# First modulation and input projection cut into quarters of the features, with idle products around them, and a new order of the early weight loads

## The reference, cut to what matters

```python
cond = jax.nn.silu(c)
mod = (cond @ ada_w + ada_b)[:, None, :]                  # ada_w is 1024 x 6144
sh1, sc1, g1, sh2, sc2, g2 = jnp.split(mod, 6, axis=-1)
h = rms_norm(x, ln1_g) * (1.0 + sc1) + sh1                # 256 x 1024
z = h @ w_in                                              # w_in is 1024 x 2840
...                                                       # attention on heads of z, then @ w_out
x = x + g1 * hybrid_mixer(...)
h = rms_norm(x, ln2_g) * (1.0 + sc2) + sh2
x = x + g2 * sparse_moe(h, ...)                           # 32 experts, top 4
```

## Time and profile before

| | |
|---|---|
| median of 3 runs | 1793.73 us (1792.29 to 1797.49) |
| the profiled execution, own time | 1794.16 us |
| its span | 1792.1 us |
| TensorE (PE) busy | 1720.9 us, 96% |
| DVE, ACT, POOL busy | 701.0, 264.4, 132.2 us |
| mean granted TensorE clock | 0.998 |
| DMA | 548.11 MB, mean 306 GB/s |

### The profile page before, as it was taken

How to read it: one execution, slowest core, us unless ns; L and a number is a source line. 1 busy time by engine, 2 the same in 40 slices (tenths; PEclk the granted TensorE clock), 3 DMA queues, 4 the chain that set the end, 5 groups by cost and what they waited for, 6 DMA issues and landing times.

```text
span 1792.1 us, 25082 instructions
## 1 busy us (share of the span) xinstructions
PE 1720.9 (96%) x10167; PEld 1057.6 (59%) x10168; DVE 701.0 (39%) x1280; ACT 264.4 (15%) x534; POOL 132.2 (7%) x188
## 2 busy tenths in 40 slices
PE   7999999999999999999999999999999999999998
PEld 4456543333333333333333333797899998899987
DVE  2655422122122121212212122664578545768743
ACT  1135211011010010101101010214111001511100
POOL 4006400000000001001010010200100000010000
PEclk9999999999999999999999999999999999999999
DMA  9988999969999999999999999741254443535440
GB/s 318 358 277 264 388 415 428 428 283 428 429 428 429 427 428 428 429 429 427 428 429 429 429 427 426 262 160 48 95 184 146 171 159 118 200 142 188 159 171 24
DMA packets 95507, 548.11 MB, mean 306 GB/s; under 512 B 6002, under 2 KB 9282, under 8 KB 68722
## 3 DMA queue, kind: packets, MB, share of 16 engines
q1 hardware_dynamic: 95298, 546.93, 76.0%
q10 hardware_dynamic: 144, 0.26, 0.0%
HBM read 546.12 MB, written 1.05 MB: 305 GB/s over the span
## 4 chain that ended last, share of the span: by engine, by line
PE 76%; DMA 19%; SPq 1%; ACT 1%; issue 1%; DVE 1%; POOL 0%; DVEq 0%; POOLq 0%; ACTq 0%
DMA ring<-in_exp_w 18%; PE ps L1312 18%; PE ps L1556 11%; PE ps L1343 8%; PE ps L1585 6%; PE ps L1626 5%; PE ps L1370 4%; PE ps L1444 4%; PE ps L971 2%; PE ps L1277 2%; PE ps L1264 2%; PE ps L1185 2%; PE ps L1655 2%; PE ps L944 1%; PE ps L1680 1%; ACT sq L1700 1%
## 5 line engine op out<-in xcount | busy, mean ns | idle before, releaser
L1312 PE MATMUL ps<-ring,sq 128*64 128x512 f32 x2112 | 464.4, 593 | 24.0 <-DMA ring<-in_exp_w 24.0
L1312 PEld LDWEIGHTS ps<-ring,sq 128*64 128x64 f32 x2112 | 146.9, 137 | 316.9 <-issue 264.0
L1343 PE MATMUL ps<-arena,sq 128*64 128x512 f32 x1056 | 233.9, 595 | 3.5
L2301 DVE TENSOR_SCALAR sq<-arena,rstd 128x64 f32<-128x64 f32 x68 | 19.5, 330 | 365.2 <-PE ps L1312 364.5
L1343 PEld LDWEIGHTS ps<-arena,sq 128*64 128x64 f32 x1056 | 75.3, 137 | 140.8 <-issue 140.5
L2374 DVE TENSOR_SCALAR hn<-ps 128x512 f32<-128x512 f32 x33 | 22.8, 692 | 318.6 <-PE ps L1312 318.6
L1807 ACT ACTIVATE sq<-hn 128x512 f32<-128x512 f32 x33 | 20.8, 629 | 528.0 <-DVE hn L2374 528.0
L1700 ACT ACTIVATE sq<-ps 128x512 f32<-128x512 f32 (+1 forms) x99 | 51.9, 524 | 308.7 <-PE ps L1343 212.2
L1556 PE MATMUL ps<-arena 128*128 128x136 f32 (+1 forms) x768 | 90.0, 277 | 0.0
L1556 PEld LDWEIGHTS ps<-arena 128*128 128x128 f32 x768 | 88.6, 191 | 0.0
L1700 ACT ACTIVATE arena<-ps 128x512 f32<-128x512 f32 (+4 forms) x68 | 33.4, 501 | 275.9 <-PE ps L1585 78.4
(11 more groups left out here) (418 smaller groups left out, 2240.1 us busy)
## 6 DMA issues: line engine op xcount, KB each, us to landing
ring<-in_exp_w SPq DMA_DIRECT2D x123, 2048.0 KB, 21.2
arena<-in_exp_w SPq DMA_DIRECT2D x68, 2048.0 KB, 19.4
ring<-in_mlp_w_up SPq DMA_DIRECT2D x16, 2048.0 KB, 7.5
ring<-in_mlp_w_down SPq DMA_DIRECT2D x16, 2048.0 KB, 7.8
ring<-in_ada_w SPq DMA_DIRECT2D x8, 2048.0 KB, 12.2
ring<-in_sb_w_qkv SPq DMA_DIRECT2D x6, 2048.0 KB, 14.5
ring<-in_w_in SPq DMA_DIRECT2D x5, 2048.0 KB, 12.2
ring<-in_ada_w SPq DMA_DIRECT2D x8, 1024.0 KB, 9.7
```

The costliest lines, as they stand in the source:

```text
L1312: last = mm(bank(2 + part)[64 * h:64 * h + 64, :], lhs, w[:, k % 2, at:at + 512], start=False, stop=(k == C - 1))
L1343: last = mm(bank(3)[64 * h:64 * h + 64, :], m.aT[:, q, 64 * half:64 * half + 64], w[:, q, 512 * h:512 * h + 512], start=(half == 0 and q = ...
```

## The change

The first modulation is computed by quarters of its columns (q = 0 to 3), each over all 1024 rows: a quarter gives scale and shift of 256 features, two chunks. Its products move 128 columns, where they moved 256. The load `mod q` brings two times 1024 rows of 256 columns. The projection's first 1304 columns (v = 0 to 5) are made by the same quarters of the features: load `inq q` holds 256 rows of `w_in` with 1304 columns, and the six banks stay open over the four quarters. Around this stand 19 idle products of the identity with itself (two before c, eight before x, four before the first modulation, two and three around its turn). VectorE instead of ACT copies the turned x out of PSUM, and ACT loads its table for the square root ahead of the squares.

The loads behind are reordered. Of group 1, parts 0 to 2 are still added up on VectorE, one after each of the third, fourth and fifth chunk of heads; part 3 goes to TensorE in `modulation_sum(1)`, in bank 1, and that sum with its turn (bank 2) moves behind `cw2`. `score(0)` now waits for the result of group 1.

```diff
-A_LOADS = ([("mod", 0, 0), ("mod", 0, 1), ("in", 0, 0), ("mod", 0, 2), ("mod", 0, 3)]
-           + [("in", 0, 1), ("in", 0, 2), ("ada", 1, 0), ("ada", 1, 1), ("in", 0, 3), ("ada", 1, 2), ("in", 0, 4),
-              ("ada", 1, 3), ("in", 0, 5), ("cmp", 0, 0)] + [("ada", 2, k) for k in range(4)] + [("wout", 0, h) for h in range(2)])
+QUARTERS = 4
+IN_FIRST = 1304
+A_LOADS = ([(kind, 0, q) for q in range(QUARTERS) for kind in ("mod", "inq")]
+           + [("in", 0, 3), ("ada", 1, 0), ("in", 0, 4), ("ada", 1, 1), ("in", 0, 5), ("cmp", 0, 0), ("ada", 1, 2),
+              ("ada", 1, 3)] + [("ada", 2, k) for k in range(4)] + [("wout", 0, h) for h in range(2)])
-MOD_BANK, MOD_TURN_BANK = (6, 7, 7), (5, 7, 7)
+MOD_BANK, MOD_TURN_BANK = (6, 1, 7), (5, 2, 7)
...
+    if kind == "inq":
+        return ("in_first", c + 1) if c < QUARTERS - 1 else ("z_done", 6)
     if (kind, layer) == ("ada", 1):
-        return "mod_added", c + 1
+        return ("mod_added", c + 1) if c < 3 else ("mod_parts", 8)
...
+    def idle_turns(count):
+        for _ in range(count):
+            mm(bank(4)[:, 0:P], ident, ident, start=True, stop=True)
+    idle_turns(2)
     pe.wait_ge(s["c_loaded"], 16)
     turn_params(bank(0), 0, C)
+    idle_turns(8)
     pe.wait_ge(s["x_loaded"], 16)
...
+    def first_modulation(q):
+        w = a_slot(A_LOADS.index(("mod", 0, q))).rearrange("p (n k f) -> p n k f", n=2, f=256)
+        for k in range(C):
             for r in range(4):
+                last = mm(bank(MOD_BANK[0])[32 * r:32 * r + 32, P * q:P * q + P], m.condR[:, k, :],
+                          w[:, r // 2, k, P * (r % 2):P * (r % 2) + P], start=(k == 0), stop=(k == C - 1))
...
     def modulation_sum(group):
-        pe.wait_ge(s["mod_added"], 4)
+        w = a_slot(A_LOADS.index(("ada", group, 3))).rearrange("p (k n) -> p k n", n=2048)
+        for kk in range(2):
+            for r in range(4):
+                mm(bank(MOD_BANK[group])[32 * r:32 * r + 32, :], m.condR[:, 6 + kk, :], w[:, kk, 512 * r:512 * r + 512],
+                   start=(kk == 0), stop=False)
+        pe.wait_ge(s["mod_added"], 3)
...
     sum_squares("squared", 0, bank(7)[:, 0:T], META, 2)
+    pe.wait_ge(s["p0_loaded"], 16 * len(PARAMS[0]))
+    turn_params(bank(0)[:, 256:512], 0, PARAM_ROWS[0])
+    idle_turns(4)
     first_modulation(0)
+    idle_turns(2)
     turn_first_modulation(0)
+    idle_turns(3)
...
+    for q in range(QUARTERS - 1):
+        for v in range(4):
+            project_quarter(v, q)
+        first_modulation(q + 1)
+        project_quarter(4, q)
+        turn_first_modulation(q + 1)
+        project_quarter(5, q).then_inc(s["in_first"], 1)
+    for v in range(6):
+        project_quarter(v, QUARTERS - 1).then_inc(s["z_done"], 1)
         if v == 1:
             turn_meta()
...
         elif v == 9:
-            modulation_sum(1)
             pe.wait_ge(s["turned_dve"], 2)
             turned_pairs(5, 0, 2)
         elif v == 10:
-            turn_modulation(1)
...
     last.then_inc(s["cmp_kv_done"], 1)
+    pe.wait_ge(s["z_copied"], 11)
+    modulation_sum(1)
...
     modulation_half(2, 0)
     modulation_half(2, 1)
+    turn_modulation(1)
...
         if u == 0:
+            pe.wait_ge(s["mod_ready"], QUARTERS + 1)
             score(0)
...
-        for part in {0: (0, 1), 2: (2,)}.get(c, ()):
-            add_modulation(part)
-        if c == 3:
+        if c == 2:
+            add_modulation(0)
+        elif c == 3:
             blocks(0, 4, 0)
             blocks(1, 5, 1)
-            add_modulation(3)
-            modulation_rows(1)
+            add_modulation(1)
         elif c == 4:
...
-            modulation(1)
+            add_modulation(2)
```

More of the change, by code:

```diff
@@ L514, in source @@
         if kind == "mod":
[L515 to L520, removed]
+            src = a["ada_w"][0].rearrange("(k p) n -> p k n", p=P)
+            at = 256 * c
+            return [(slice(0, P), 2048, 256, src[:, :, at + D * n:at + D * n + 256]) for n in range(2)]
+        if kind == "inq":
+            src = a["w_in"][0, 256 * c:256 * c + 256, 0:IN_FIRST]
+            return [(slice(0, P), 2 * IN_FIRST, IN_FIRST, src.rearrange("(k p) n -> p k n", p=P))]
         if kind == "in":
@@ L871, in sum_squares, with turn_first_modulation @@
         last.then_inc(s["norm_summed"], 1)
[L873 to L877, removed]
+    def first_modulation(q):
+        w = a_slot(A_LOADS.index(("mod", 0, q))).rearrange("p (n k f) -> p n k f", n=2, f=256)
+        for k in range(C):
             for r in range(4):
-                last = mm(bank(MOD_BANK[0])[32 * r:32 * r + 32, 256 * h:256 * h + 256], m.condR[:, 4 * rows + k, :],
-                          w[:, r // 2, k, 256 * (r % 2):256 * (r % 2) + 256],
-                          start=(rows == 0 and k == 0), stop=(rows == 1 and k == 3))
+                last = mm(bank(MOD_BANK[0])[32 * r:32 * r + 32, P * q:P * q + P], m.condR[:, k, :],
+                          w[:, r // 2, k, P * (r % 2):P * (r % 2) + P], start=(k == 0), stop=(k == C - 1))
         last.then_inc(s["mod_parts"], 1)
-    def turn_first_modulation(h):
-        pe.wait_ge(s["mod_rows"], h + 1)
-        for q in range(2):
-            at = 256 * h + P * q
-            last = turn(bank(MOD_TURN_BANK[0])[:, at:at + P], m.modrow[:, at:at + P], ident)
-        last.then_inc(s["mod_turned"], 1)
+    def turn_first_modulation(q):
+        pe.wait_ge(s["mod_rows"], q + 1)
+        turn(bank(MOD_TURN_BANK[0])[:, P * q:P * q + P], m.modrow[:, P * q:P * q + P], ident).then_inc(s["mod_turned"], 1)
     def modulation_half(group, half):
         k, kk = half // 2, half % 2
-        if group == 2 and half == 0:
-            pe.wait_ge(s["mod_ready"], 3)
         w = a_slot(A_LOADS.index(("ada", group, k))).rearrange("p (k n) -> p k n", n=2048)
@@ L1006, in compressed_hidden @@
         last.then_inc(s["cmp_hidden"], 1)
-    for v in range(4, 12):
+    for v in range(6, 12):
         pe.wait_ge(s["z_copied"], v - 3)
@@ L1703, in program_scalar @@
     f(m.sig, m.prm[:, PC_C:PC_C + C], ACT.Sigmoid).then_inc(s["sig_ready"], 1)
-    for b in range(4):
-        act.wait_ge(s["x_turned"], b + 1)
-        copy(m.xT[:, 2 * b:2 * b + 2, META:TT], bank(1 + b).rearrange("p (c t) -> p c t", c=2), "x_placed")
+    nc.scalar.preload_act_table(ACT.Sqrt)
     for b in range(4):
         act.wait_ge(s["x_placed"], b + 1)
-        xs = m.xT[:, 2 * b:2 * b + 2, META:TT]
-        f(m.sq[:, 2 * b:2 * b + 2, META:TT], xs, ACT.Square).then_inc(s["squared"], 1)
+        f(m.sq[:, 2 * b:2 * b + 2, META:TT], m.xT[:, 2 * b:2 * b + 2, META:TT], ACT.Square).then_inc(s["squared"], 1)
     act.wait_ge(s["norm_summed"], 1)
@@ L2055, in first_modulation @@
         v.tensor_tensor(dst, src, bias, ALU.add).then_inc(s["mod_ready"], 1)
[L2056 to L2060 removed]
+        dve.wait_ge(s["mod_ready"], q + 1)
+        link(v.scalar_tensor_tensor(m.affine[:, pair], m.modT[:, M_SC1 + 2 * q:M_SC1 + 2 * q + 2], 1.0,
+                                    col(PC_LN1 + 2 * q, 2), ALU.add, ALU.mult))
@@ L2069, in program_vector @@
+    for b in range(4):
+        dve.wait_ge(s["x_turned"], b + 1)
+        v.tensor_copy(m.xT[:, 2 * b:2 * b + 2, META:TT], bank(1 + b).rearrange("p (c t) -> p c t", c=2)).then_inc(
+            s["x_placed"], 1)
+    dve.wait_ge(s["prm_turned"], 2)
+    v.tensor_copy(m.prm[:, C:PARAM_ROWS[0]], bank(0)[:, 256 + C:256 + PARAM_ROWS[0]]).then_inc(s["prm_ready"], 1)
     dve.wait_ge(s["x_placed"], 4)
```

102 lines of the change are left out of this document (42 added, 60 removed).

## The result

| | before | changed kernel |
|---|---|---|
| median of 7 runs each, same chip | 1793.01 us (1791.96 to 1797.49) | 1797.41 us (1796.88 to 1799.81) |
| profiled execution, own time and span | 1794.16 and 1792.1 us | 1798.75 and 1797.0 us |
| TensorE busy, mean granted clock | 1720.9 us, 0.998 | 1730.3 us, 0.996 |

The ratio is 1.0027 with a 95% interval of 1.0017 to 1.0037: 4.4 us slower, on the near side of the 0.3% that counts as a change here. The forecast was 1797.3. That the two agree to 0.1 us is partly luck: the kernel before came out 0.7 lower here than in the three runs that the forecast started from (1793.01 against 1793.73), and the difference was 4.4 us where +3.55 was forecast. The traced execution of the changed kernel took 1.3 us more than the median of that kernel, the traced one before 1.2 more than its own.

A forecast was written before the change was run, and what follows sets the result against it. TensorE bounds the kernel until the attention loop ends, then the DMA stream of expert weights. Terms -4.7 + 1.45 + 7.2 - 0.4 = +3.55 us gave a median of 1797.3 us, range 1788 to 1803, likeliest case 1795 to 1799.

The forecast's parts named there:

- The bound: Before 166.7 us: time won or lost on TensorE moves the start of the expert-weight stream and reaches the run's end whole.
- The front: From the start to the first projection: it starts at 18.5 us, 4.7 earlier, bounds 17.0 and 21.4.
- The waits of 0.3 us in each quarter: Before the projection of a quarter: TensorE waits 0.3 us for the first chunk, three times.
- slow turns and sums: At the front: if idle products don't raise the clock, sums end at 14 and not about 12, costing 1.2 us.
- v = 6 to the turn of the GELU: Third addition on VectorE ahead of the GELU makes TensorE wait 2.9 us; net +1.45.
- a load of the same size took 10.9 us before: Weights of VectorE's third addition, issued at z_done 10 behind `cmp`, take 10.9 us to land.
- To score(0): From z_done 12 to score(0): +7.2 us, of it 3.7 waiting for the first part of group 2, issued only at z_done 12.
- The moved sum: Group 1's sum with its new part, behind `cw2` on TensorE: 1.9 + 1.0 us, 2.9 of the +7.2 to score(0).
- rival (c): Narrow modulation products decide, slower: 64 rows at 60 ns, +6.6, time 1803.9; clock falling in two waits adds 1 to 2; chance 0.20.
- The first round: First round of the attention loop: wait 1.0 us for a load, but 5.5 at full clock; taken as -0.4.
- The wait of 1.0 for the third load: First round: group 2's part for pieces 4 and 5, third load in a row, lands 18.1 after z_done 12, wanted at 17.15.
- Rival (b): Late loads land sooner, 8.3 us and not 10.9: -2.6, front at 17.0 another -1.5; 1793.2 us, from 1789 to 1794.7; chance 0.20.

The follow-up runs named there:

- e12: e9 plus three idle products in the pause ahead of the scores of the compressed keys: 1789.34 us, ratio to the kernel before 0.9979.
- e8: The changed kernel without any of its 19 idle products: 1801.39 us, +8.26 to the kernel before.
- e2: The changed kernel with VectorE's third addition of group 1 moved behind the GELU: 1795.28 us, +1.58 to the kernel before.
- e3: The changed kernel with the loads of group 1's parts brought forward and VectorE's additions moved ahead of the GELU: 1793.30 us, -0.40 to the kernel before.
- e5: e3 with the four loads of expert biases behind the compression weights instead of ahead: 1789.96 us, -3.17 to the kernel before, ratio 0.9981.
- e6: e5 with part 3 of group 1 added by VectorE instead of by TensorE's products: 1790.30 us, -2.83 to the kernel before.
- e7: e2 with 14 idle products filling TensorE's wait for the first part of group 2: 1795.20 us, +2.07 to the kernel before.
- e1: The changed kernel without the nine idle products around the first modulation: 1798.15 us, +4.45 to the kernel before.
- e4: The changed kernel with 14 idle products filling TensorE's wait for the first part of group 2: 1796.75 us, +3.05 to the kernel before.
- e11: The kernel before with only the ten idle products at its very start added: 1792.68 us, -0.86 to the kernel before.
- e9: e5 with the first small parameters issued ahead of `mod 0` and without the four idle products behind them: 1789.81 us, -3.73 to the kernel before.

## Why the prediction was right, and where it was not

**The bound: right.** What moves the start of the stream moves the end. In all fourteen traces the end of the span lies 1625.2 to 1626.1 us behind that start, while the start itself goes from 161.55 (e12) to 175.10 (e8).

**The front: right, with three sizes off.** `mod` came at 350 GB/s (over 7 to 11 us), where 343 was predicted:

```profile
7.00:11.00 4.00, 3.77 (x25) 3.41 (x25) 2.48 (x4) 2.17 (x4) 3.46 (x7) 1.00 1.10 350
```

So runs of 1 KB are again below the 376 and more of longer ones, which speaks against the rule of the Trainium skill (DMA: Bandwidth & Descriptors, Specifications) that 512 B give the full rate. (The 5.6 us that I worked out by that rule took 376 GB/s for the full rate; at the 428 of the earlier trace rows it is an estimate of 4.9 us.) The first projection stood at 18.43 for 18.5, and that close only because errors offset each other: the modulation began at 14.61 and not at 13.95, but was shorter, and from its end to the projection were 1.9 us and not 2.4. A quarter of the modulation took 1.95 us, the low bound, and not 2.2: 30.5 ns a row of 128 columns. The sums ended at 13.3 and not at 12; part of it is that the eight idle products ran past the landing of x (the turns started at 7.11, x was there by 6.25 in the kernel before). The waits of 0.3 us in each quarter did not come, and v = 6 was 5.03 and not 4.7 us sooner. That slow turns and sums would cost 1.2 us fits the 1.0 of e8 at its first projection; what I had not seen is that the waits then grow and the projection itself runs at half the clock for a while, 3 us more.

**v = 6 to the turn of the GELU: mechanism right, size wrong.** The step "a load of the same size took 10.9 us before" was the mis-sized term: it took 9.5 here, so the wait was 1.52 and not 2.9, and the net 0.04 and not +1.45 (issues at 90.5 to 91.3 us):

```profile
ring<-in_ada_w SPq DMA_DIRECT2D x1, 2048.0 KB, 9.5
```

That it is VectorE's order is shown by e2.

**To score(0): mechanism right, one term missing.** The first part of group 2 landed 7.5 us after its issue and not 8.3, so the wait was 3.00 and not 3.7 (issues at 111.5 to 111.8 us):

```profile
ring<-in_ada_w SPq DMA_DIRECT2D x1, 2048.0 KB, 7.5
```

e3 and e5 show that the place of its issue makes this wait. The moved sum is on the path at 2.7 us (111.90 to 114.61), 2.9 predicted; e6 shows that VectorE could not take its new part without giving 1.3 of the 1.9 back. The missing term is the clock. I had it only in rival (c), where it "would add 1 to 2" for the two waits together. With the wait filled, `cw2` (109.73) to `score(0)` (122.67) took 12.9 us in e7; in the changed kernel 15.5. So it cost 2.6 at this place in the traced execution, which is one from above the median; in that of e1, which is one from below, it cost some 1.6.

**The first round: wrong by 0.5.** I had full clock there (-0.4), but it was at half for more than half of its 6.0 us; the difference is +0.08. The wait of 1.0 for the third load did not come here, where the products ahead of it ran slowly; in e4 and e7, which reach that place sooner, it came (1.17 and 1.05).

**The sum.** Three waits or durations came out smaller (1.4, 0.7, 0.3 us) and the clock 2.6 + 0.5 larger; they cancel to +0.7 at the start of the stream, and a further 0.6 lies behind that start, within the 0.9 by which the fourteen traces differ there. Rival (b) had the right sign for the loads but it was too small to win; (c) is refuted in its main form, 64 rows at 60 ns.

**Left open.** What brings the fall of the clock is not settled. It fell behind every one of the four pauses of 3.0 us (changed kernel, e1, e2, e8), at the end of one of 2.18 us in e11, and about the second of two close together, 1.62 and 1.04 us, in e8. It did not fall behind 2.17 us ahead of v = 6 in the kernel before, behind 2.28 us in e3, nor behind this one at the GELU in e8, after which the clock was whole until 124:

```profile
112.57 0.33 PE L1041 MATMUL ps<-ident,arena 128*128 128x128 f32 x1 [2.71 <-DVE arena L2161]
```

So the length of the pause alone does not decide. Behind the scores, which follow a pause of 0.57 to 0.65 us, it fell in the kernel before, e1, e4 to e9 and e11 and not in e2 and e3 (in the changed kernel it was at half already); with that pause filled it did not fall in two traces of two, and the mean clocks of the 22 runs agree.

## What to carry to other kernels

Time won ahead of a queue of loads is lost again if the next load is issued on an event and not as soon as a slot could be free: look at what frees the slot before counting a gain. When a wait on TensorE is priced, give the sum with the products behind it at half the clock too, and at the next wait again: it came in some traces here and not in others. A wait that the trace puts down to "issue" may be a load: take its issue time and its time to landing and see whether they add up to the end of the wait.

## What the runs showed of the hardware that was not expected

- Behind the same pause of 3.0 us the clock was at half from 120.5 to 130.7 us in the changed kernel, and in e1 only between 119 and 123. There the two pieces of group 2 took 3.35 us instead of 1.92 and the scores their 1.97, a loss of some 1.6 us with the turn, against 2.6 here.
- Idle products ahead of the first real work brought 16 turns from 3.68 to 1.91 us in most of the traces and to 2.27 to 2.63 in some. The granted clock reads 1.00 in either case, so in these traces the column does not tell what the start of the kernel costs.
- Products of 128 columns in four groups of 32 output rows follow each other at 30.5 ns a row; cost stayed proportional to columns from 512 (120 ns) over 256 (60 ns) down to 128.
- 0.9 MB of biases on 32 partitions each, queued ahead of a load that is waited for, cost 2.3 us there (e3); queued behind it they made no wait (e5).
